# A two-block mixing and transformer kernel: banks, order of work and one late tile at the joints between stages

## The reference, cut to what matters

```python
def second_block(x, p, ...):
    h = x
    for i in range(2):
        h = h + 0.5 * swiglu(rmsnorm(h, g_ff1[i]), w_ff1_in[i], w_ff1_out[i])
        h = h + hybrid_mixer(rmsnorm(h, g_mix[i]), ...)
        h = h + 0.5 * swiglu(rmsnorm(h, g_ff2[i]), w_ff2_in[i], w_ff2_out[i])
        gate = jax.nn.sigmoid(rmsnorm(h, g_ple[i]) @ w_ple_gate[i])
        h = h + gate * (p[i] @ w_ple_proj[i])
    return rmsnorm(h, g_final)

def hybrid_mixer(u, w_in, b_f, w_attn_out, conv_w, conv_b, g_conv, w_conv_out, w_out):
    z = u @ w_in
    q, k, v, f_logit, glu_in, gate_a, gate_c = split(z)
    y_attn = forgetting_attention(q, k, v, f_logit + b_f) @ w_attn_out
    y_conv = conformer_conv(glu_in, conv_w, conv_b, g_conv) @ w_conv_out
    merged = sigmoid(gate_a) * y_attn + sigmoid(gate_c) * y_conv
    return merged @ w_out
```

## Time and profile before

| | |
|---|---|
| median of three runs | 3125.68 us (3123.44 to 3134.28) |
| profiled execution, own time | 3129.88 us |
| its span | 3128.1 us, 51785 instructions |
| TensorE (PE) busy | 3016.4 us, 96% |
| TensorE weight loads (PEld) | 2574.9 us, 82% |
| VectorE (DVE) busy | 2104.8 us, 67% |
| ScalarE (ACT) busy | 1422.2 us, 45% |
| GpSimd (POOL) busy | 479.0 us, 15% |
| mean granted TensorE clock | 0.989 of full speed |

### The profile page before, as it was taken

The page is one execution under the profiler, slowest core; times in us unless marked ns, Lnnn a source line. Parts: engine busy times, 40 slices in busy tenths (PEclk is TensorE's granted clock), DMA queues, the critical chain, the costliest instruction groups (busy, mean ns, idle before and its releaser), DMA issues.

```text
span 3128.1 us, 51785 instructions
## 1 busy us (share of the span) xinstructions
PE 3016.4 (96%) x19012; PEld 2574.9 (82%) x19012; DVE 2104.8 (67%) x3101; ACT 1422.2 (45%) x2295; POOL 479.0 (15%) x392
## 2 busy tenths in 40 slices
PE   7999999999999999999999999999999999999998
PEld 4788888887799988667789987799887667799986
DVE  5665665446699745776699844899447776799635
ACT  3655555453366523334456622566323334466422
POOL 0213223075600010000200012100110000200012
PEclk9999999999999999999999999999999999999998
DMA  6112021123223222212323223233322112223321
GB/s 247 51 51 60 13 62 43 39 85 111 90 106 105 98 95 79 68 61 68 101 94 105 103 95 107 72 104 107 102 80 81 62 61 80 101 95 106 108 99 69
DMA packets 94911, 270.91 MB, mean 87 GB/s; under 512 B 35440, under 2 KB 36592, under 8 KB 93424
## 3 DMA queue, kind: packets, MB, share of 16 engines
q1 hardware_dynamic: 94016, 267.89, 25.6%
q0 software_dynamic: 320, 1.05, 0.1%
q10 hardware_dynamic: 432, 0.02, 0.0%
HBM read 263.68 MB, written 5.24 MB: 86 GB/s over the span
## 4 chain that ended last, share of the span: by engine, by line
PE 83%; DVE 7%; ACT 4%; issue 2%; SPq 2%; DMA 1%; ACTq 0%; DVEq 0%
PE bank L149 15%; PE bank L151 15%; PE bank L150 15%; PE bank L2027 8%; PE bank L2028 8%; PE bank L2029 8%; PE bank L2523 1%; PE bank L1599 1%; PE bank L2544 1%; ACT weights_hi L137 1%; SPq L665 1%; DVE weights_lo L142 1%; PE bank L1613 1%; PE bank L1665 1%; PE bank L2533 1%
## 5 line engine op out<-in xcount | busy, mean ns | idle before, releaser
L142 DVE TENSOR_TENSOR weights_lo<-weights_raw,weights_hi 128x1024 fp32r<-128x1024 f32 (+2 forms) x258 | 397.0, 1539 | 361.1 <-ACT weights_hi L137 356.9
L137 ACT ACTIVATE weights_hi<-weights_raw 128x1024 fp32r<-128x1024 f32 (+2 forms) x250 | 285.3, 1141 | 470.5 <-PE bank L151 457.5
L149 PE MATMUL bank<-x_hi,weights_hi 128*128 128x512 f32 x832 | 335.7, 403 | 9.6 <-DVE x_lo L1915 3.1
L151 PE MATMUL bank<-x_hi,weights_lo 128*128 128x512 f32 x832 | 327.9, 394 | 0.0
L150 PE MATMUL bank<-x_lo,weights_hi 128*128 128x512 f32 x832 | 327.8, 394 | 0.0
L2027 PE MATMUL bank<-sum_hi,block_hi 128*128 128x256 f32 x960 | 272.0, 283 | 4.1 <-ACT bank L2179 3.7
L150 PE MATMUL bank<-hidden_lo,weights_hi 128*128 128x512 f32 x704 | 273.9, 389 | 0.0
L149 PE MATMUL bank<-hidden_hi,weights_hi 128*128 128x512 f32 x704 | 273.9, 389 | 0.0
L151 PE MATMUL bank<-hidden_hi,weights_lo 128*128 128x512 f32 x704 | 273.9, 389 | 0.0
L2028 PE MATMUL bank<-sum_lo,block_hi 128*128 128x256 f32 x960 | 271.6, 283 | 0.0
L2029 PE MATMUL bank<-sum_hi,block_lo 128*128 128x256 f32 x960 | 270.2, 282 | 0.0
(11 more groups left out here) (454 smaller groups left out, 7510.8 us busy)
## 6 DMA issues: line engine op xcount, KB each, us to landing
raw_pair<-w_ff1in SPq DMA_DIRECT2D x42, 1024.0 KB, 4.8
raw_pair<-w_ff2in SPq DMA_DIRECT2D x42, 1024.0 KB, 4.9
weights_raw<-w_mix SPq DMA_DIRECT2D x72, 512.0 KB, 3.2
weights_raw<-w_ff1out SPq DMA_DIRECT2D x32, 704.0 KB, 4.0
weights_raw<-w_ff2out SPq DMA_DIRECT2D x32, 704.0 KB, 4.1
weights_raw<-w_tail SPq DMA_DIRECT2D x42, 512.0 KB, 3.3
mod_weights<-w_mod SPq DMA_DIRECT2D x6, 2048.0 KB, 16.1
weights_raw<-w_dn SPq DMA_DIRECT2D x24, 512.0 KB, 3.6
```

Source lines behind the costliest of these rows:

```text
L137: nc.scalar.activation(K.wh[:, slot, 0:cols], K.raw[:, slot, 0:cols], ACT.Copy).then_inc(S.wh_ready, 1)
L142: nc.vector.tensor_tensor(K.wl[:, slot, 0:cols], K.raw[:, slot, 0:cols], K.wh[:, slot, 0:cols].bitcast(F32), ALU.subtract).then_inc(S.raw_ ...
L149: nc.tensor.matmul(out, K.wh[:, slot, a:b], xh, start=start, stop=False)
L151: return nc.tensor.matmul(out, K.wl[:, slot, a:b], xh, start=False, stop=stop)
```

## The change

1. `c`: slab 0 writes bank 3 instead of bank 0. Slab 2 therefore waits only for what slab 1 waits for (`evac` v0 + 2), not for the reading of slab 0. Slabs 2 and 3 are written out, and the loop starts at pair 2.
2. `at`, VectorE: the reading of slab 0 (`mixed_out(0)`, the first queries) runs ahead of the end of the forget chain, and the low weights of slab 2 stay behind the chain.
3. `at`, VectorE: `logits(0)` runs ahead of the third group of four taps.
4. `am`: ScalarE makes the four convolved high parts ahead of the high weights of slab 29, and TensorE waits for each convolved tile by itself.
5. `wo`: TensorE does units 0 to 6 of slab 0, units 0 to 3 of slab 1, then unit 7 of slab 0 (the last merged tile), then the rest of slab 1.
6. `ple`: tile 0 writes banks 4 and 6 instead of 0 and 2. Tile 2 waits only for what tile 1 waits for. Tiles 2 and 3 are written out.

```diff
-    def pe_project(pe, s, v, slot, q=None):
+    def pe_project(pe, s, v, slot, bank=None):
...
-            if q is not None:
-                pe.wait_ge(S.xg_ready, 8 * q + k + 1)
-            last = mm3(pb[slot][:, :], slot, k, xgh[:, k, :], xgl[:, k, :], k == 0, k == 7)
+            last = mm3(pb[slot if bank is None else bank][:, :], slot, k, xgh[:, k, :], xgl[:, k, :], k == 0, k == 7)
...
-        pe_project(pe, s0, v0, 0)
+        pe_project(pe, s0, v0, 0, 3)
         pe_sum_squares(pe, q)
         pe_project(pe, s0 + 1, v0 + 1, 1)
-        with pe.Fori(1, 4) as i:
+        pe_project(pe, s0 + 2, v0 + 1, 0)
+        pe_project(pe, s0 + 3, v0 + 3, 1)
+        with pe.Fori(2, 4) as i:
...
-            if first:
-                pe.wait_ge(S.cv_ready, 4 * (l + 1))
             for k in range(4):
+                if first:
+                    pe.wait_ge(S.cv_ready, 4 * l + k + 1)
                 last = mm3(pb[2 + slot][:, :], slot, 4 + k, K.cv_h[:, k, :], K.cv_l[:, k, :], k == 0, k == 3)
...
-        wo(0, 0, True)
-        wo(1, 1, False)
+        pe.wait_ge(S.raw_read, s4 + 1 + CREDIT)
+        pe.wait_ge(S.evac, v4 + 1)
+        for k in range(7):
+            pe.wait_ge(S.mg_ready, 8 * l + k + 1)
+            wo_tile(0, k)
+        pe.wait_ge(S.raw_read, s4 + 2 + CREDIT)
+        pe.wait_ge(S.evac, v4 + 2)
+        for k in range(4):
+            wo_tile(1, k)
+        pe.wait_ge(S.mg_ready, 8 * l + 8)
+        wo_tile(0, 7).then_inc(S.slab_done, 1)
+        for k in range(4, 8):
+            last = wo_tile(1, k)
+        last.then_inc(S.slab_done, 1)
...
-        split_hi(act, s1 + 29, 1, 1024)
         for t in range(4):
             act.wait_ge(S.cs_ready, 4 * l + t + 1)
             nc.scalar.activation(K.cv_h[:, t, :], K.cy[:, t, :], ACT.Copy).then_inc(S.cvh_ready, 1)
+        split_hi(act, s1 + 29, 1, 1024)
...
-            nc.vector.tensor_tensor(K.glu[:, i, 30:542], pb[0][:, :], rstd[:, :], ALU.mult).then_inc(S.evac, 1)
+            nc.vector.tensor_tensor(K.glu[:, i, 30:542], pb[3 if first else 0][:, :], rstd[:, :], ALU.mult).then_inc(S.evac, 1)
...
-        slab_out(0)
+        dve.wait_ge(S.slab_done, s1 + 1 + CREDIT)
+        mixed_out(0)
+        dve.wait_ge(S.fln_ready, l + 1)
...
+        split_lo(dve, s1 + 2, 0, 1024)
         taps(4)
         slab_out(1)
         taps(4)
         slab_out(2)
+        logits(0)
         taps(4)
-        logits(0)
...
-        tile(0, 0, True)
+        tile(0, 0, True, at=4)
         pe_sum_squares(pe, q)
         tile(1, 1, False)
-        with pe.Fori(1, 4) as i:
+        tile(2, 0, False, v0 + 2)
+        tile(3, 1, False)
+        with pe.Fori(2, 4) as i:
```

More of the change, by code:

```diff
@@ L2596, in mix_pe, with wo_tile, wo @@
         s4, v4 = K.slab(l, "wo"), K.evic(l, "wo")
-        def wo(m, slot, first):
+        def wo_tile(slot, k):
+            return mm3(pb[slot][:, :], slot, k, K.mg_h[:, k, :], K.mg_l[:, k, :], k == 0, k == 7)
+        def wo(m, slot):
             pe.wait_ge(S.raw_read, s4 + m + 1 + CREDIT)
@@ L2601, in wo @@
             for k in range(8):
-                if first:
-                    pe.wait_ge(S.mg_ready, 8 * l + k + 1)
-                last = mm3(pb[slot][:, :], slot, k, K.mg_h[:, k, :], K.mg_l[:, k, :], k == 0, k == 7)
+                last = wo_tile(slot, k)
             last.then_inc(S.slab_done, 1)
-        wo(0, 0, True)
-        wo(1, 1, False)
+        pe.wait_ge(S.raw_read, s4 + 1 + CREDIT)
[12 more added lines that the diff above has]
+        last.then_inc(S.slab_done, 1)
         with pe.Fori(1, 4) as i:
             for slot in range(2):
-                wo(2 * i + slot, slot, False)
+                wo(2 * i + slot, slot)
     def mix_act(act, l):
@@ L2782, in mix_dve, with mixed_out @@
             glu(i, False)
[L2783 to L2789, removed]
         s1, v1 = K.slab(l, "at"), K.evic(l, "at")
-        def slab_out(t):
-            split_lo(dve, s1 + t + 2, t % 2, 1024)
+        def mixed_out(t):
             kind, i = mixer_slab(t)
@@ L2804, in slab_out @@
             ins.then_inc(S.evac, 1)
+        def slab_out(t):
+            split_lo(dve, s1 + t + 2, t % 2, 1024)
+            mixed_out(t)
         def logits(n):
@@ L2828, in attended @@
                 .then_inc(S.ao_ready, 1)
-        slab_out(0)
+        dve.wait_ge(S.slab_done, s1 + 1 + CREDIT)
+        mixed_out(0)
+        dve.wait_ge(S.fln_ready, l + 1)
+        chain.link(nc.vector.tensor_tensor(K.fx[R, :], K.fx[R, :], K.fe[R, :], ALU.subtract))
+        chain.link(nc.vector.tensor_tensor_scan(K.fc[R, :], K.onerow[R, :], K.fx[R, :], 0.0, ALU.mult, ALU.add))
+        chain.link(nc.vector.tensor_copy(K.fch[R, :], K.fc[R, :]))
+        nc.vector.tensor_tensor(K.fcl[R, :], K.fc[R, :], K.fch[R, :].bitcast(F32), ALU.subtract).then_inc(S.cm_ready, 1)
+        chain.leave(LAYERS, FCHAIN)
+        hold(dve, S)
+        split_lo(dve, s1 + 2, 0, 1024)
         taps(4)
@@ L2922, in ple_pe, with tile @@
         s0, v0 = K.slab(l, "ple"), K.evic(l, "ple")
-        def tile(m, slot, first):
+        def tile(m, slot, first, freed=None, at=0):
             pe.wait_ge(S.raw_read, s0 + m + 1 + CREDIT)
-            pe.wait_ge(S.evac, v0 + m + 1)
+            pe.wait_ge(S.evac, v0 + m + 1 if freed is None else freed)
             if first:
@@ L2929, in tile @@
             for k in range(2):
-                mm3(pb[2 + slot][:, :], slot, 8 + k, K.p_h[:, k, :], K.p_l[:, k, :], k == 0, k == 1)
+                mm3(pb[at + 2 + slot][:, :], slot, 8 + k, K.p_h[:, k, :], K.p_l[:, k, :], k == 0, k == 1)
             for k in range(8):
@@ L2933, in tile @@
                     pe.wait_ge(S.xg_ready, 8 * q + k + 1)
-                last = mm3(pb[slot][:, :], slot, k, xgh[:, k, :], xgl[:, k, :], k == 0, k == 7)
+                last = mm3(pb[at + slot][:, :], slot, k, xgh[:, k, :], xgl[:, k, :], k == 0, k == 7)
             last.then_inc(S.slab_done, 1)
-        tile(0, 0, True)
+        tile(0, 0, True, at=4)
         pe_sum_squares(pe, q)
         tile(1, 1, False)
-        with pe.Fori(1, 4) as i:
+        tile(2, 0, False, v0 + 2)
+        tile(3, 1, False)
+        with pe.Fori(2, 4) as i:
             for slot in range(2):
@@ L2986, in ple_dve, with scaled, gated @@
         s0, v0 = K.slab(l, "ple"), K.evic(l, "ple")
-        def scaled(m, slot):
+        def scaled(m, slot, at=0):
             dve.wait_ge(S.slab_done, s0 + m + 1 + CREDIT)
             dve.wait_ge(S.gu_ready, 8 * l + m + CREDIT)
-            nc.vector.tensor_tensor(K.t1[:, :], pb[slot][:, :], rstd[:, :], ALU.mult).then_inc(S.gt_ready, 1)
-        def gated(m, slot):
+            nc.vector.tensor_tensor(K.t1[:, :], pb[at + slot][:, :], rstd[:, :], ALU.mult).then_inc(S.gt_ready, 1)
+        def gated(m, slot, at=0):
             n = 8 * l + m
             dve.wait_ge(S.gs_ready, n + 1)
-            nc.vector.tensor_tensor(K.t2[:, :], K.silu[:, :], pb[2 + slot][:, :], ALU.mult).then_inc(S.gu_ready, 1)
+            nc.vector.tensor_tensor(K.t2[:, :], K.silu[:, :], pb[at + 2 + slot][:, :], ALU.mult).then_inc(S.gu_ready, 1)
             dve.wait_ge(S.gu_ready, n + 1 + CREDIT)
@@ L3003, in tile @@
                 dve_rstd(dve, q, v0)
-            scaled(m, slot)
-            gated(m, slot)
+            scaled(m, slot, 4 if first else 0)
+            gated(m, slot, 4 if first else 0)
         tile(0, 0, True)
```

## The result

The changed kernel takes 3108.7 us (median of four runs, 3104.3 to 3111.6) where the kernel before takes 3127.6 us (median of four): the ratio is 0.9936, with a 95% interval of 0.9914 to 0.9959. The forecast was 3109, with 3102 to 3118. The profiled execution is the quickest of the four: 3104.3 us, span 3102.5 us, mean granted clock 0.994 (before 0.989).

The account below looks back on a forecast made before the run. TensorE, busy 96% of the span, bounds the kernel; only its stalls and half clock can be won. Stalls 11.8 us plus clock 6.6 make 18.4 us, giving 3111.5 profiled, 3107.3 median, forecast 3109; 8 in 10 within 3102 to 3118.

Parts of the forecast that it names:

- Mixing: Mixing stage, slab 2: TensorE's 1.12 us stall for bank 0 goes, slab 4 stays covered; 2.2 us in two layers.
- Queries: First attention queries: read before the forget chain, so TensorE waits only for the low weights; 0.6 us, two layers 1.2.
- Logits: First attention probabilities: logits run beside the taps, probabilities still behind them; 0.4 us a layer, 0.8 in two, about 0.85 idle left.
- Convolved parts: Convolved tiles: the stall of 1.7 us goes and the weights moved behind stay hidden; 3.4 us in two layers.
- Late tile: Output slabs: the merged-tile wait goes, but TensorE waits 2.5 us for low weights at the third slab; gain 0.
- a split that starts first: Output stage, shared memory port: a split starting before GpSimd would end about 1 us earlier, making the new stall 1.5 us.
- Embedding: Embedding stage, tile 2: the 2.08 us stall goes and tile 3 has 0.5 us of cover; 4.2 us in two layers.
- Clock: Half-clock stretches behind embedding and probabilities stalls: four go, 1.65 us each, 6.6 us; bounds 0 and 9.9.
- a stretch that was forecast to stay: Output slabs: the new 2.5 us stall should draw half clock as the 1.99 us one did, so no clock gain there.
- The 4.2 us between the profiled execution and the median: Profiled execution becomes 3111.5, median run 3107.3; how much of the difference is half clock was unknown, so the middle: 3109.

Follow-up runs that it names:

- the second set of runs: The changed kernel run once more, unaltered, for its spread and clock, against the kernel before: 3110.6 us, ratio 0.9943 (0.9929 to 0.9957).
- the weights first: Changed kernel, with ScalarE splitting the next weights before the gain and VectorE their low parts before x_lo, in two output-stage turns: 3104.7 us, ratio 0.9922.

## Why the prediction was right, point by point

**Mixing, 2.2 us.** Right: the wait for `glu` is gone, with the cover at slab 4 holding.

**Queries, 1.2 us.** Right in kind. TensorE is released by the low weights; the idle fell from 1.10 to 0.37, two layers 1.5 us.

**Logits, 0.8 us.** The mechanism held and the size was low: the idle fell from 1.25 to 0.60, two layers 1.3 us. The step that was mis-sized is "taps end 0.28 later, ... then 0.5 for reciprocal and product", which put 3.6 us between the start of the logits and the end of the probabilities. Measured it is 1260.97 + 0.29 - 1257.92 = 3.34 us: the taps start 0.20 us after the logits, and four taps, reciprocal and product take 3.14 us, as rows that overlap in part.

**Convolved parts, 3.4 us.** Right, and the weights moved behind made nobody wait.

**Late tile, 0.** Right, and close in size: 2.5 us of wait forecast at the third slab, 2.2 to 2.4 of recorded idle, and 2.38 and 2.36 found. The split of the low weights took 2.17 us beside GpSimd's sum, as forecast from 2.19. What the prediction adds on a split that starts first is not tested: in no run does it start ahead of all of GpSimd's work.

**Embedding, 4.2 us.** Right; TensorE does not wait at tile 3.

**Clock, 6.6 us: the size came out, the places did not.** Each run reports its mean granted clock c. Span times (1 - c) is the time lost at half clock where TensorE is the bound, span times c the rest. The mean span and c over 58 runs of the kernel before are 3125.6 and 0.9898: 31.7 lost, 3093.9 the rest. Over nine runs of the changed kernel they are 3107.5 and 0.9920: 24.9 lost, 3082.6 the rest. Of each loss 7 to 8 us lie in the last 15 us of the span, where the clock is 0.50 and TensorE is busy for only 3.9 us; that is in both kernels and falls out of the difference. So the stalls gave about 11.3 us (forecast 11.8) and the clock about 6.9 (forecast 6.6); c is given to 0.001, and the two sets of the changed kernel differ by 2.8 us in what they lose, so these are good to 1 or 2 us.

That the clock came out so near is partly luck. The prediction read each stretch as belonging to its stall. Twelve profiles show how often that holds: the kernel before and the five with a single part of the change, and six of the changed kernel and its variants.

| stall | idle, us | with half clock behind it |
|---|---|---|
| embedding, `h` | 1.92 | 10 of 10 |
| last merged tile | 1.99 to 2.30 | 10 of 12 |
| third output slab, low weights | 2.36 to 2.38 | 3 of 6, layer 0 each time |
| first probabilities | 1.24 to 1.25 | 3 of 10 |
| convolved tile | 1.54 | 0 of 10 |
| second feed-forward, untouched | 1.92 to 1.93 | 16 of 24 |

The two stretches in the embedding stage are the sure part of the forecast: where the stall is gone, 14 places in seven profiles, the half clock is gone too. The two at the probabilities were counted from the one profile that has both; the others have one in eight. In their place the changed kernel's two profiles lack a stretch that was forecast to stay (output slabs, layer 1) and one that the prediction never named (second feed-forward, layer 0). Why an unchanged stall there loses its stretch is open. The profile that the prediction read was also the one with the most half clock: 34.1 us from the first mixing stage to the last embedding tile, where the five kernels with a single part of the change have 20.5 to 27.3 and the changed kernel 13.7 in both of its profiles.

**Sum.** The five parts, each alone, give 3.8, 6.9, 4.4, 4.7 and 0.3 us by their ratios, 20.0 together; the whole change gives 20.0 by its ratio and 18 by the second set of runs. They add within the noise: each part is known to 3 us either way, so their sum to about 6. The waits in the profiles say the same without that noise, since each edit alone removes its own row, or moves it, and leaves the others.

**The 4.2 us between the profiled execution and the median** I halved without a reason from the rows. With more runs the kernel before has medians of 3127.1 to 3127.7, close to the middle that I had taken; that too is luck.

## What to carry to other kernels

When the bound engine waits at a joint, follow the work behind the awaited one too: the late tile removed a wait of 2 us and made one of 2.4 us one slab later, because the tile's end releases a weight buffer and the chain from that release (gain, split, low parts) was longer than the work left to hide it. Moving the tile took TensorE's waits down only together with shortening that chain (2.38 us to 0.40), and shortening it is a change of order on ScalarE and VectorE. Before a small edit is judged by time, its joint is read in the profile: the waits at these joints repeat to 0.1 us, where the time of single executions of one kernel spreads over 3 to 15 us. A half-clock stretch is not counted from one profile: it can be missing from the next, behind the same stall.

## What the runs showed of the hardware

- Stalls of nearly one size are followed by half clock in one place and not in another, in both of two executions: 2.38 us in layer 0 drew it, 2.36 us in layer 1 did not; 1.25 us did at the probabilities in the kernel before, and in the kernel with the mixing bank alone did not. In the first block, which no edit touches, the places change from one execution to the next. That fits the rule of the Trainium skill (TensorE: Matmul & The Clock Gate, The HAM clock gate) that the gate's observation runs freely against the kernel; why layers 0 and 1 repeat in the two executions is left open.
- In one trace, keeping TensorE busy with matmuls that nobody needs kept the clock at 1.00 through a stall (0.50 and 0.55 without them), but cost and gained nothing that the time shows.
- VectorE's subtraction of 128x1024 took 1.23 us alone and 2.17 us when it started 0.69 us behind the start of GpSimd's sum of squares. With the weights first it started beside GpSimd's squares, 0.79 us ahead of the sum, and took 1.79 us; the sum then took 2.16 us instead of 1.77. In both kernels the subtraction ends 1.08 to 1.09 us after the GpSimd instruction that was running when it started (1520.36 and 1521.45 us; 1525.33 and 1526.41 us), as if it had stood until that one was done. That is two cases, and a reading of the rows, not a test.
